# One of four weight sums of a quad made by two transfers instead of by VectorE

## The chip, the cores and the metric

The kernel runs on one core of a Trainium2 chip. The metric is the device time of one execution in microseconds (us). Before the change it is 1186.18 us, the median of two executions (1186.14 and 1186.23).

## What is computed

The reference is one layer of an encoder over 512 tokens of width 1024: a first feed-forward block, a mixer (attention beside an mLSTM), a second feed-forward block and a gated embedding. The change touches only the two feed-forward blocks:

```python
def swiglu(x, w_gate, w_up, w_down):
    return (jax.nn.silu(x @ w_gate) * (x @ w_up)) @ w_down

u = rmsnorm(h, ffn1_pre_norm[i])
h = h + 0.5 * rmsnorm(swiglu(u, ffn1_w_gate[i], ffn1_w_up[i], ffn1_w_down[i]), ffn1_post_norm[i])
# ... mixer ..., then the same with the ffn2 weights
```

w_gate and w_up are 1024 x 2816 and w_down is 2816 x 1024, all float32.

## The kernel before

**Precision.** Each float32 factor is split in two parts for TensorE: a high part (`w_hi`, a copy rounded by ScalarE) and a low part (`w_lo`, the difference, made by VectorE). A product is three matmuls, high by high, high by low and low by high.

**A feed-forward block** is built by `ffn`, called once for each block. Its gate and up weights are worked off in 11 pairs of 256 columns. The first two pairs (`LEADS`) are multiplied plainly. The other nine give 18 "quads", one of gate columns and one of up columns for each pair: 36 quads in the kernel. `w_down` follows.

**A quad** is a product of 2 x 2 blocks in the manner of Strassen and Winograd, with seven block products instead of eight. The weights of a quad lie in two slots of `w_raw`, one transfer of 512 KB each: the first holds rows 0 to 511 of 256 columns, the second rows 512 to 1023. `raw_blocks` names A11 and A21, the two column halves of the first slot, and A12 and A22, those of the second. Each is 128 partitions by 512 elements, 256 KB. VectorE makes four sums of them in `wsum` (`sum_dve`, lines 971 to 977):

S1 = A21 + A22, S3 = A11 - A21, S2 = S1 - A11, S4 = A12 - S2.

The operands of the seven products come in four groups g. Group 0 is A11, group 1 the whole second slot (A12 and A22), group 2 is S1 and S2, group 3 is S3 and S4. For each group ScalarE makes the high part (`group_hi`, line 910) and VectorE the low part (`group_lo`, line 923), in the order 0, 2, 3, 1. TensorE multiplies in `block_pe` (lines 781 to 783), seven products of 12 matmuls of 256 columns, and waits before its products for `s_lo` (low parts done) and `rcopy` (copies by ScalarE between banks): products 2 and 3 need group 2, product 4 group 1, products 5 and 6 group 3, product 7 group 1 and the fourth copy of its quad.

**The order on each engine is written out by hand**, and each engine works its queue in order. While TensorE multiplies quad qd, the other engines prepare quad qd + 1:

- VectorE (`dve_prog`): `group_lo` 0, then the sums S1, S3, S2 and S4, `group_lo` 2, three results of quad qd (lines 990 to 1001), `group_lo` 3, one more result, `close_dve`, `group_lo` 1.
- ScalarE (`act_prog`): copy 1 of quad qd, `group_hi` 0, copies 2 and 3, `group_hi` 2, which waits for S2, copy 4, `group_hi` 3, `group_hi` 1.
- SP (`sp_prog`, line 742) issues the two raw loads of quad qd + 2 as soon as all sums (`s_dve`) and low parts (`s_lo`) of quad qd are made.
- GpSimd (`pool_prog`) adds squares and makes `vraw` before the first quad (lines 593 to 596 and 1123) and has nothing to do in the quads.

Of the kernel before, what the change touches and what calls it, by code (L numbers as in the profile page):

```python
# [22 lines left out]
ALU = mybir.AluOpType  # L23
# [6 lines left out]
P = 128  # L30
# [29 lines left out]
LEADS = 2  # L60
# [60 lines left out]
def program(nc, w, const, out):  # L121
    ctx = ExitStack()
    with ctx:
        block_build(nc, w, const, out, ctx)


def block_build(nc, w, const, out, ctx):
# [151 lines left out]
    class Boundary:  # L279

        signals = Signals("boundary")
        PER = {"y_ready": (8, 7, 1, 7, 0), "y_copied": (0, 8, 8, 8, 0), "ysq_act": (0, 8, 8, 8, 8),
               "y_acc": (0,) + tuple(ADDED.values()), "y_sum": (0, 1, 1, 1, 1), "r1_ready": (0, 2, 1, 1, 1), "r1_root": (0, 1, 0, 0, 1), "r1b_ready": (0, 1, 1, 1, 1),
               "h_ready": (8,) * 5, "vhi_ready": (8,) * 5, "v_ready": (8,) * 5, "hsq_ready": (8,) * 5,
               "h_acc": (8,) * 5, "h2_ready": (1,) * 5, "r2_ready": (1,) * 5, "r2b_ready": (1,) * 5,
               "rb_ready": (1,) * 5, "t_ready": (0, 8, 8, 8, 0), "h_kept": (0, 8, 8, 8, 0)}
# [7 lines left out]
        def wait(self, eng, name, value):  # L294
            eng.wait_ge(self.signals[name], sum(self.PER[name][:self.n]) + value)

# [68 lines left out]
    def hi_upto(act, n):  # L365
        while hi_next[0] <= min(n, CHUNKS - 1):
            split_hi(act, hi_next[0])
            hi_next[0] += 1
# [219 lines left out]
    def h_squares_pool(pool, n, beside=None):  # L588
        b = bs[n]
        for m in range(KD):  # L590
            b.wait(pool, "hsq_ready", m + 1)
            if m == 0:
                nc.gpsimd.tensor_copy(sqacc[:], scratch[:, 0, :]).then_inc(b["h_acc"], 1)
            else:
                b.wait(pool, "h_acc", m)
                nc.gpsimd.tensor_tensor(sqacc[:], sqacc[:], scratch[:, m % 4, :], ALU.add).then_inc(b["h_acc"], 1)
            if beside is not None and m < 5:
                beside(m)
        if beside is not None:
            for m in range(5, KD):  # L600
                beside(m)
# [78 lines left out]
    class Block:  # L680

        signals = Signals("ffn")
        PAIRS = NI - LEADS
        PER = {"mm": 14 * PAIRS, "post": 8 * PAIRS, "rcopy": 8 * PAIRS, "s_dve": 8 * PAIRS, "s_hi": 8 * PAIRS,
               "s_lo": 8 * PAIRS, "lead_out": 4 * LEADS, "gate_scaled": NI, "silu_done": NI, "prod_ready": NI, "phi": KF,
               "plo": KF, "vraw_ready": KD, "t_raw": 4, "t_hi": 4, "t_lo": 4}

# [6 lines left out]
        def before(self, name):  # L694
            return self.n * self.PER[name]

# [3 lines left out]
    def ffn(n, N, DN, wg, wu, wd, pre):  # L700
        own = Block(n // 2)
        yb = bs[n + 1]
        QUADS = 2 * (NI - LEADS)
# [8 lines left out]
        def halves(ap):  # L712
            return ap.rearrange("p (k c) -> p k c", k=4)

        def raw_blocks(q):

            a, b = (halves(w_raw[:, (N + 2 * q + e) % RING, :]) for e in range(2))
            return a[:, :, 0:P], b[:, :, 0:P], a[:, :, P:2 * P], b[:, :, P:2 * P]

        def raw_loaded(qd, e):  # L720

            j = 2 * (qd % 2) + e
            return w_loaded[(N + j) % RING], LOADED[N + 4 * (LEADS - 1) + j] + 16 * (qd // 2 + 1)
# [13 lines left out]
        def sp_load(sp, i, j):  # L737

            m = N + j
            up, half = (j // 2, j % 2) if i > 0 else (j % 2, j // 2)  # L740
            src = (wu if up else wg)[0, half * 512:half * 512 + 512, i * 256:i * 256 + 256]
            sp.dma_start(w_raw[:, m % RING, :].rearrange("p (k c) -> p k c", k=4),
                         src.rearrange("(k p) c -> p k c", p=P)).then_inc(w_loaded[m % RING], 16)

        def sp_prog(sp, loaded=0, after_lead=None):
            for j in range(loaded, 4):
                if N + j >= RING:
                    sp.wait_ge(w_lo_done, N + j - RING + 1)
                sp_load(sp, 0, j)
            if after_lead is not None:  # L750
                after_lead(sp)
            for i in range(1, NI):
                for j in range(4):
                    if i <= LEADS:
                        sp.wait_ge(w_lo_done, N + 4 * (i - 1) + j + 1)
                    else:
                        qd = 2 * (i - LEADS - 1) + j // 2
                        own.wait(sp, "s_dve", 4 * qd + 4)
                        own.wait(sp, "s_lo", 4 * qd + 4)
                    sp_load(sp, i, j)  # L760
            for k in range(KF):
                m = DN + k
                if k < RING:
                    qd = QUADS - 2 + k // 2
                    own.wait(sp, "s_dve", 4 * qd + 4)
                    own.wait(sp, "s_lo", 4 * qd + 4)
                else:
                    sp.wait_ge(w_lo_done, m - RING + 1)
                sp.dma_start(w_raw[:, m % RING, :], wd[0, k * P:k * P + P, :]).then_inc(w_loaded[m % RING], 16)
# [114 lines left out]
        def group_ap(g, q):  # L884

            if g == 1:
                return w_raw[:, (N + 2 * q + 1) % RING, :], slice(0, CH)
            if g == 0:
                return raw_blocks(q)[0], slice(0, CH // 2)
            return wsum[:, 2 * g - 4:2 * g - 2, :, :].rearrange("p a k c -> p (a k c)"), slice(0, CH)  # L890

        S1, S2, S3, S4 = (wsum[:, a, :, :] for a in range(4))

        def group_hi(act, qd, g):

            if qd == QUADS:
                if g == 0:
                    hi_upto(act, DN)
                return
            if g < 2:  # L900
                act.wait_ge(*raw_loaded(qd, g))
            else:
                own.wait(act, "s_dve", 4 * qd + g + 1)
            if qd == 0:
                act.wait_ge(w_used, N + 4 * (LEADS - 1) + g + 1)
            else:
                own.wait(act, "mm", 7 * (qd - 1) + FREED[g])
            src, c = group_ap(g, qd % 2)
            o = w_hi[:, (N + g) % RING, c]
            nc.scalar.activation(halves(o) if g == 0 else o, src, ACT.Copy).then_inc(own["s_hi"], 1)  # L910
# [50 lines left out]
        def sum_dve(dve, qd, e):  # L961

            if qd == QUADS:
                return
            A11, A12, A21, A22 = raw_blocks(qd % 2)
            if e == 0:
                for r in range(2):
                    dve.wait_ge(*raw_loaded(qd, r))
                if qd >= 1:
                    own.wait(dve, "s_lo", 4 * (qd - 1) + 3)  # L970
                nc.vector.tensor_tensor(S1, A21, A22, ALU.add).then_inc(own["s_dve"], 1)
                nc.vector.tensor_tensor(S3, A11, A21, ALU.subtract).then_inc(own["s_dve"], 1)
                own.wait(dve, "s_dve", 4 * qd + 1)
                nc.vector.tensor_tensor(S2, S1, A11, ALU.subtract).then_inc(own["s_dve"], 1)
            else:
                own.wait(dve, "s_dve", 4 * qd + 3)
                nc.vector.tensor_tensor(S4, A12, S2, ALU.subtract).then_inc(own["s_dve"], 1)

        t0, t1 = slice(0, 256), slice(256, 512)
# [97 lines left out]
        def act_prog(act, late=None, arena_free=None):  # L1077
# [9 lines left out]
            if arena_free is not None:  # L1087
                arena_free(act)
            bs[n].wait(act, "h_acc", KD)
            group_hi(act, 0, 0)  # L1090
            lead_out_act(act, 1, 0)
            group_hi(act, 0, 2)
            silu_act(act, 1)
            group_hi(act, 0, 3)
            group_hi(act, 0, 1)
            lead_out_act(act, 1, 1)
# [23 lines left out]
        def pool_prog(pool):  # L1120

            def keep_raw(m):
                nc.gpsimd.tensor_tensor(vraw[:, m, :], h[:, m, :], pre(m).broadcast_to([P, S]), ALU.mult).then_inc(own["vraw_ready"], 1)

            h_squares_pool(pool, n, keep_raw)

        def y_wait(eng, p):
            if p < KD - 1:
                yb.wait(eng, "y_ready", p + 1)
            else:  # L1130
                eng.wait_ge(w_used, DN + KF)

        return sp_prog, pe_prog, dve_prog, act_prog, y_wait, sp_load, pool_prog

    f1 = ffn(0, UP1, DN1, w["ffn1_w_gate"], w["ffn1_w_up"], w["ffn1_w_down"], lambda m: col("ffn1_pre_norm", m))
    f2 = ffn(2, UP2, DN2, w["ffn2_w_gate"], w["ffn2_w_up"], w["ffn2_w_down"], lambda m: col("ffn2_pre_norm", m))

    def half_post(a):
# [1082 lines left out]
    block = ctx.enter_context(nc.Block())  # L2221
# [277 lines left out]
```

## Time and profile before

| | |
|---|---|
| median of the runs | 1186.18 us |
| the profiled execution | 1183.95 us |
| its span, first to last instruction | 1182.2 us |
| TensorE busy | 1170.5 us, 99% of the span |
| VectorE busy | 817.8 us, 69% |
| ScalarE busy | 582.5 us, 49% |
| GpSimd busy | 131.0 us, 11% |
| moved by transfers | 111.99 MB, mean 95 GB/s |
| mean granted TensorE clock | 0.996 of full speed |

The profile names an instruction by its line in the kernel, its engine, its operation and its tiles. Matmuls overlap, so their busy times add up to more than the time in which they follow each other. What an engine waited for stands behind its idle time. For transfers the profile gives the time from the issue on the queue to the landing of the last byte.

### The profile page before, as it was taken

To read this page: it belongs to the slowest core of one execution; us is meant where nothing else is said; L and a number is where in the kernel's file an instruction comes from. 1 tells how busy PE (TensorE), PEld (TensorE's weight loads), DVE (VectorE), ACT (ScalarE), POOL (GpSimd) and SP (SyncE) were. 2 spreads that over 40 slices of the span, in tenths; PEclk is the share of its full clock that TensorE was granted. 3 is DMA by queue.
4 is the path that set the end of the run, shared out by engine and by line. 5 is a ranking of instruction groups with operands and counts; after the bars stand their busy time and mean duration, and the time that the engine had idled before them with its cause. 6 is when DMAs were issued, how large, how long until landed. Compare 5 with 4: busy or idle time off the path is not lost.

```text
span 1182.2 us, 17769 instructions
## 1 busy us (share of the span) xinstructions
PE 1170.5 (99%) x6860; PEld 1009.6 (85%) x6860; DVE 817.8 (69%) x1309; ACT 582.5 (49%) x921; POOL 131.0 (11%) x111
## 2 busy tenths in 40 slices
PE   9999999999999999999999999999999999999998
PEld 8899999988888886667887888789999998888887
DVE  6888888773337787665466874688888886333574
ACT  6555555533236437666333623565555554323473
POOL 6000000000014000001022201430000000000344
PEclk9999999999999999999999999999999999999998
DMA  6233333342231331111532233322333334232211
GB/s 210 86 107 106 107 107 106 112 138 90 96 93 36 90 107 53 37 38 49 146 89 72 86 111 107 98 81 72 107 106 107 107 106 143 89 106 90 89 37 72
DMA packets 101854, 111.99 MB, mean 95 GB/s; under 512 B 15294, under 2 KB 91678, under 8 KB 101542
## 3 DMA queue, kind: packets, MB, share of 16 engines
q1 hardware_dynamic: 97542, 109.18, 29.8%
q10 hardware_dynamic: 4256, 2.12, 0.6%
q8 instruction: 29, 0.48, 0.2%
q14 instruction: 27, 0.22, 0.1%
HBM read 108.12 MB, written 3.16 MB: 94 GB/s over the span
## 4 chain that ended last, share of the span: by engine, by line
PE 91%; DVE 4%; ACT 3%; issue 2%; DMA 1%; SPq 0%; POOL 0%; ACTq 0%; DVEq 0%
PE bank L303 14%; PE bank L305 14%; PE bank L304 14%; PE bank L781 10%; PE bank L782 10%; PE bank L783 10%; PE bank L626 2%; PE bank L620 2%; PE bank L621 2%; PE bank L310 1%; PE bank L312 1%; PE bank L311 1%; PE bank L1366 1%; PE bank L455 1%; PE bank L1345 1%
## 5 line engine op out<-in xcount | busy, mean ns | idle before, releaser
L337 DVE TENSOR_TENSOR w_lo<-w_raw,w_hi 128x1024 fp32r<-128x1024 f32 x121 | 155.9, 1298 | 173.6 <-ACT w_hi L330 173.3
L330 ACT ACTIVATE w_hi<-w_raw 128x1024 fp32r<-128x1024 f32 x121 | 125.9, 1054 | 191.9 <-PE bank L305 183.1
L781 PE MATMUL bank<-T_hi,w_hi 128*128 128x256 f32 x576 | 163.1, 283 | 1.2 <-ACT bank L1075 1.2
L782 PE MATMUL bank<-T_lo,w_hi 128*128 128x256 f32 x576 | 163.0, 283 | 0.0
L783 PE MATMUL bank<-T_hi,w_lo 128*128 128x256 f32 x576 | 163.0, 283 | 0.0
L303 PE MATMUL bank<-T_hi,w_hi 128*128 128x512 f32 x352 | 137.3, 390 | 0.0
L304 PE MATMUL bank<-T_lo,w_hi 128*128 128x512 f32 x352 | 137.0, 389 | 0.0
L305 PE MATMUL bank<-T_hi,w_lo 128*128 128x512 f32 x352 | 137.0, 389 | 0.0
L303 PE MATMUL bank<-v_hi,w_hi 128*128 128x512 f32 x328 | 132.7, 405 | 0.0
L305 PE MATMUL bank<-v_hi,w_lo 128*128 128x512 f32 x328 | 128.2, 391 | 0.0
L304 PE MATMUL bank<-v_lo,w_hi 128*128 128x512 f32 x328 | 127.8, 390 | 0.0
L783 PE MATMUL bank<-v_hi,w_lo 128*128 128x256 f32 x432 | 122.3, 283 | 0.0
L782 PE MATMUL bank<-v_lo,w_hi 128*128 128x256 f32 x432 | 122.3, 283 | 0.0
L781 PE MATMUL bank<-v_hi,w_hi 128*128 128x256 f32 x432 | 122.2, 283 | 0.0
L923 DVE TENSOR_TENSOR w_lo<-wsum,w_hi 128x1024 fp32r<-128x1024 f32 x72 | 88.3, 1226 | 43.8 <-ACT w_hi L910 43.8
L910 ACT ACTIVATE w_hi<-wsum 128x1024 fp32r<-128x1024 f32 x72 | 76.4, 1061 | 83.2 <-PE bank L783 38.4
L781 PEld LDWEIGHTS bank<-T_hi,w_hi 128*128 128x128 f32 x576 | 110.6, 192 | 1.6 <-issue 1.6
L782 PEld LDWEIGHTS bank<-T_lo,w_hi 128*128 128x128 f32 x576 | 110.6, 192 | 0.0
L783 PEld LDWEIGHTS bank<-T_hi,w_lo 128*128 128x128 f32 x576 | 110.6, 192 | 0.0
L782 PEld LDWEIGHTS bank<-v_lo,w_hi 128*128 128x128 f32 x432 | 82.9, 192 | 0.1
L781 PEld LDWEIGHTS bank<-v_hi,w_hi 128*128 128x128 f32 x432 | 82.9, 192 | 0.1
L783 PEld LDWEIGHTS bank<-v_hi,w_lo 128*128 128x128 f32 x432 | 82.9, 192 | 0.0
(311 smaller groups left out, 2333.5 us busy)
## 6 DMA issues: line engine op xcount, KB each, us to landing
w_raw<-in_ffn_w_up SPq DMA_DIRECT2D x44, 512.0 KB, 4.0
w_raw<-in_ffn_w_down SPq DMA_DIRECT2D x44, 512.0 KB, 3.5
w_raw<-in_ffn_w_gate SPq DMA_DIRECT2D x43, 512.0 KB, 4.0
w_raw<-in_w_in SPq DMA_DIRECT2D x32, 512.0 KB, 3.7
w_raw<-in_w_out SPq DMA_DIRECT2D x8, 512.0 KB, 3.4
w_raw<-in_ple_w_gate SPq DMA_DIRECT2D x8, 512.0 KB, 3.4
x_tm<-in_x SPq DMA_DIRECT2D x4, 512.0 KB, 7.6
Mb<-m_rows ACTq DMA_DIRECT2D x8, 256.0 KB, 4.9
```

The costliest lines, as they stand in the source:

```text
L303: nc.tensor.matmul(o, whi, a_hi, start=start, stop=False)
L304: nc.tensor.matmul(o, whi, a_lo, start=False, stop=False)
L305: return nc.tensor.matmul(o, wlo, a_hi, start=False, stop=stop)
L330: nc.scalar.activation(w_hi[:, s, :], w_raw[:, s, :], ACT.Copy).then_inc(w_hi_done, 1)
L337: nc.vector.tensor_tensor(w_lo[:, s, :], w_raw[:, s, :], w_hi[:, s, :].bitcast(F32), ALU.subtract).then_inc(w_lo_done, 1)
L620: nc.tensor.matmul(o[:], whi, v_hi[:, k, :], start=(k == 0), stop=False)
L621: nc.tensor.matmul(o[:], wlo, v_hi[:, k, :], start=False, stop=False)
L781: nc.tensor.matmul(o, whi, a_hi(kk), start=(start and kk == 0), stop=False, skip_group_check=True)
L782: nc.tensor.matmul(o, whi, a_lo(kk), start=False, stop=False, skip_group_check=True)
L783: last = nc.tensor.matmul(o, wlo, a_hi(kk), start=False, stop=(kk == 3), skip_group_check=True)
L910: nc.scalar.activation(halves(o) if g == 0 else o, src, ACT.Copy).then_inc(own["s_hi"], 1)
L923: nc.vector.tensor_tensor(o, src, hh, ALU.subtract).then_inc(own["s_lo"], 1)
```

## The change

S1 is no longer made by VectorE. GpSimd issues two transfers for each quad. The first copies A21 from the weights in HBM to the place of S1 in `wsum`. GpSimd waits until it has landed and issues the second, which reads A22 from HBM and adds it to what lies in S1 (`accum_op=ALU.add`). Both move 256 KB in rows of 128 float32. Before the first one GpSimd waits until the low part of group 2 of the quad before is made (the last reader of the old S1 and S2) and until its S2 is made. VectorE now makes S3 first and then waits for the landing of the second transfer (`s_acc`) before S2. The count of `s_dve` for each quad falls from four to three, and the waits on it are renumbered.

```diff
-        PER = {"mm": 14 * PAIRS, "post": 8 * PAIRS, "rcopy": 8 * PAIRS, "s_dve": 8 * PAIRS, "s_hi": 8 * PAIRS,
+        PER = {"mm": 14 * PAIRS, "post": 8 * PAIRS, "rcopy": 8 * PAIRS, "s_dve": 6 * PAIRS, "s_acc": 32 * PAIRS, "s_in": 32 * PAIRS, "s_hi": 8 * PAIRS,
...
-                        own.wait(sp, "s_dve", 4 * qd + 4)
+                        own.wait(sp, "s_dve", 3 * qd + 3)
...
-                own.wait(act, "s_dve", 4 * qd + g + 1)
+                own.wait(act, "s_dve", 3 * qd + g)
...
                 if qd >= 1:
                     own.wait(dve, "s_lo", 4 * (qd - 1) + 3)
-                nc.vector.tensor_tensor(S1, A21, A22, ALU.add).then_inc(own["s_dve"], 1)
                 nc.vector.tensor_tensor(S3, A11, A21, ALU.subtract).then_inc(own["s_dve"], 1)
-                own.wait(dve, "s_dve", 4 * qd + 1)
+                own.wait(dve, "s_acc", 16 * qd + 16)
                 nc.vector.tensor_tensor(S2, S1, A11, ALU.subtract).then_inc(own["s_dve"], 1)
             else:
-                own.wait(dve, "s_dve", 4 * qd + 3)
+                own.wait(dve, "s_dve", 3 * qd + 2)
                 nc.vector.tensor_tensor(S4, A12, S2, ALU.subtract).then_inc(own["s_dve"], 1)
...
             h_squares_pool(pool, n, keep_raw)
+
+            def block(qd, half):
+                i = LEADS + qd // 2
+                src = (wu if qd % 2 else wg)[0, half * 512:half * 512 + 512, i * 256 + P:i * 256 + 2 * P]
+                return src.rearrange("(k p) c -> p k c", p=P)
+
+            for qd in range(QUADS):
+                if qd >= 1:
+                    own.wait(pool, "s_lo", 4 * (qd - 1) + 2)
+                    own.wait(pool, "s_dve", 3 * (qd - 1) + 2)
+                pool.dma_start(S1, block(qd, 0)).then_inc(own["s_in"], 16)
+                own.wait(pool, "s_in", 16 * qd + 16)
+                pool.dma_start(S1, block(qd, 1), accum_op=ALU.add).then_inc(own["s_acc"], 16)
```

## Rows read from the trace of the kernel before

**Rows 1.** The page: the span, and busy time by engine

```profile
span 1182.2 us, 17769 instructions
PE 1170.5 (99%) x6860; PEld 1009.6 (85%) x6860; DVE 817.8 (69%) x1309; ACT 582.5 (49%) x921; POOL 131.0 (11%) x111
```

**Rows 2.** The page: the chain that ended last, shares by engine

```profile
PE 91%; DVE 4%; ACT 3%; issue 2%; DMA 1%; SPq 0%; POOL 0%; ACTq 0%; DVEq 0%
```

**Rows 3.** Waits: who waited for whom, us in total, times, longest

```profile
PE bank L781 <- ACT bank L1075: 1.2, 2, 0.6
...
ACT w_hi L910 <- DVE wsum L974: 31.6, 34, 1.6
```

**Rows 4.** Windows: busy us of each engine in a stretch, PEclk, DMA share, GB/s

```profile
57.00:238.00 181.00, 180.38 (x1503) 180.20 (x1503) 155.84 (x229) 101.27 (x155) 0.00 (x0) 1.00 0.33 108
```

**Rows 5.** Groups of instructions: S1's line, count, busy us, mean ns

```profile
L971 DVE TENSOR_TENSOR wsum<-w_raw 128x512 f32<-128x512 f32 x36 | 24.6, 684 | 0.0
```

**Rows 6.** Timeline of VectorE in the first block: start us, us, line, [idle before]

```profile
124.40 1.23 DVE L923 TENSOR_TENSOR w_lo<-wsum,w_hi 128x1024 fp32r<-128x1024 f32 x1 [0.40 <-ACT w_hi L910]
...
129.73 1.82 DVE L923 TENSOR_TENSOR w_lo<-w_raw,w_hi 128x1024 fp32r<-128x1024 f32 x2
131.47 0.68 DVE L971 TENSOR_TENSOR wsum<-w_raw 128x512 f32<-128x512 f32 x1
132.07 0.69 DVE L972 TENSOR_TENSOR wsum<-w_raw 128x512 f32<-128x512 f32 x1
132.67 0.68 DVE L974 TENSOR_TENSOR wsum<-wsum,w_raw 128x512 f32<-128x512 f32 x1
133.39 0.69 DVE L977 TENSOR_TENSOR wsum<-w_raw,wsum 128x512 f32<-128x512 f32 x1
134.48 1.23 DVE L923 TENSOR_TENSOR w_lo<-wsum,w_hi 128x1024 fp32r<-128x1024 f32 x1 [0.40 <-ACT w_hi L910]
```

**Rows 7.** Timeline of ScalarE: group 2's high part, fourth copy, group 3's

```profile
123.31 1.06 ACT L910 ACTIVATE w_hi<-wsum 128x1024 fp32r<-128x1024 f32 x1 [0.89 <-DVE wsum L974]
124.93 0.37 ACT L1075 ACTIVATE bank<-bank 128x256 f32<-128x256 f32 x1 [0.56 <-PE bank L783]
126.43 1.06 ACT L910 ACTIVATE w_hi<-wsum 128x1024 fp32r<-128x1024 f32 x1 [1.13 <-PE bank L783]
```

**Rows 8.** Timelines of GpSimd and VectorE around the first quads of both blocks

```profile
26.44 5.01 POOL L1123 TENSOR_TENSOR vraw<-h,cols 128x512 f32<-128x512 f32 x3
50.20 0.69 DVE L974 TENSOR_TENSOR wsum<-wsum,w_raw 128x512 f32<-128x512 f32 x1
53.15 1.22 DVE L923 TENSOR_TENSOR w_lo<-wsum,w_hi 128x1024 fp32r<-128x1024 f32 x1
62.79 0.69 DVE L974 TENSOR_TENSOR wsum<-wsum,w_raw 128x512 f32<-128x512 f32 x1
...
776.62 4.02 POOL L1123 TENSOR_TENSOR vraw<-h,cols 128x512 f32<-128x512 f32 x3
799.25 0.68 DVE L974 TENSOR_TENSOR wsum<-wsum,w_raw 128x512 f32<-128x512 f32 x1
```

**Rows 9.** `Mb` (eight transfers issued by ScalarE, 256 KB each): time to landing

```profile
DMA to landing us min/median/max: 3.2/4.9/7.4
```

**Rows 10.** DMA queues, 569 to 582 us: packets, MB, share of 16 engines

```profile
q10 hardware_dynamic: 3618, 1.81, 49.1%
```

**Rows 11.** SP's issue of two raw loads, and their queue, 131 to 136 us

```profile
131.02 1.08 SPq L742 DMA_DIRECT2D w_raw<-in_ffn_w_up  x2
...
q1 hardware_dynamic: 1056, 1.05, 63.1%
```

**Rows 12.** Windows, columns as in Rows 4, around a fall of the clock

```profile
1106.00:1110.00 4.00, 3.99 (x28) 3.31 (x26) 1.48 (x3) 1.69 (x3) 1.25 (x1) 1.00 0.11 14
1110.00:1115.00 5.00, 5.00 (x20) 4.07 (x20) 3.41 (x14) 2.00 (x3) 0.00 (x0) 0.66 0.79 303
```

**Rows 13.** DMA issues: transfer, count, KB each, median us to landing

```profile
x_tm<-in_x SPq DMA_DIRECT2D x4, 512.0 KB, 7.6
```

More of the change, by code:

```diff
@@ L764, in sp_prog @@
                     qd = QUADS - 2 + k // 2
-                    own.wait(sp, "s_dve", 4 * qd + 4)
+                    own.wait(sp, "s_dve", 3 * qd + 3)
                     own.wait(sp, "s_lo", 4 * qd + 4)
```

## The prediction

> **What bounds the kernel now.** I read the busy times first. TensorE is busy for 1170.5 of 1182.2 us [rows 1], and the chain that ended last runs over it for 91% [rows 2]. The windows of the first block's quads say the same: 180.38 of 181.00 us, at full clock, while VectorE has 155.84, ScalarE 101.27 and GpSimd nothing [rows 4]. The waits say what is left to win: TensorE waited 1.2 us in two places for ScalarE's copies, in all 36 quads [rows 3]. One quad takes 10.08 us, from the low part of group 2 at 124.40 to the same at 134.48 [rows 6]. So VectorE is not the limit of the quads, and relief for it can only pay if it shortens something TensorE waits for.
>
> **What is removed.** 36 additions of 684 ns [rows 5]. They follow each other every 0.60 us [rows 6], so VectorE gets back 0.60 us for each quad, 21.6 us in all. ScalarE's high part of group 2 does wait for S2, 31.6 us in all [rows 3], and would start up to 0.6 us earlier. But its low part is finished at 125.63 (124.40 + 1.23). TensorE begins product 7 of the running quad when group 3's high part is let go, at about 126.4 [rows 7]; a product lasts 10.08 / 7 = 1.44 us, so product 2 of the next quad, the first that needs group 2, comes at 126.4 + 2.88 = 129.3, 3.6 us later. TensorE's own queue hides all of it. Worth: 0 us. Without that cover it would be at most those 21.6 us. The renumbered waits cost nothing, since the same instructions release them.
>
> **What is added, and what it lies beside.** GpSimd may issue the first transfer for the next quad when the low part of group 2 is made, at 125.63 us [rows 6]. The sum is wanted when S2 starts, at 132.67, or at 132.07 now that S1's slot on VectorE is gone. So there are 7.04 us in which the two transfers cost nothing; call what they take together, from the first issue to the second landing, L. They can't overlap, since the second waits for the first.
>
> If L is longer, a loop closes that has nothing of TensorE in it: low part of group 2, first transfer, second transfer, S2, high part of group 2, low part of group 2. Outside the transfers it takes 3.04 us (132.67 to 134.48 + 1.23 = 135.71) [rows 6]. The quad then takes L + 3.04 us instead of 10.08, so each one is late by L - 7.04.
>
> The first quad of a block escapes: GpSimd ends its last piece at 31.45 and S2 follows at 50.20; in the second block it is 780.64 and 799.25, over 18.6 us each time [rows 8]. The second quad has 62.79 - 54.37 = 8.42 us [rows 8], 1.38 more than the others. 17 quads of each block pay.
>
> **What is queued behind the wait.** On VectorE, S2, S4, the low part of group 2 and the results of the running quad stand behind it. On ScalarE, the high part of group 2 waits for S2, and behind that is the fourth copy, which TensorE needs for product 7 of the *running* quad. That is the first thing to be late. The copy starts at 124.93 and takes 0.37; product 7 starts about when group 3's high part is let go, 126.43; the high part of group 2 ends 0.56 us before the copy [rows 7]. So it may come 0.56 + 1.13, some 1.7 us later, once for each block, before TensorE stands. The raw loads on SP's queue go out when the quad before is finished, two quads ahead, and get later with it; they are not in the loop. GpSimd's queue holds nothing else until the quads are over.
>
> **The price of the transfers.** The trace shows no transfer issued by GpSimd and none that adds. Nearest in size, in rows of 512 bytes and in source are the eight that fill `Mb`: 3.2 us at the shortest, 4.9 in the median, 7.4 at the longest [rows 9]. For the first transfer I take the median, since preparing 512 pieces by GpSimd should cost more than the shortest case. The second must also read what it adds to. `Mb`'s queue had the 16 engines busy for 49.1% of 13 us with 3618 packets, 28.2 ns of one engine for a packet, so 512 packets take 0.9 us [rows 10]; I add that once. It also meets the raw loads. They are issued at 131.02, 5.4 us after the first transfer, and keep the engines busy for 63.1% of 5 us, 3.15 us [rows 11]. The second transfer starts at about 4.9 and shares the engines with them; I take half, 1.6 us. So the second takes 4.9 + 0.9 + 1.6 = 7.4 and L = 12.3 us. Below it is bounded by 3.2 + 3.2 + 0.9 = 7.3 us, above by the four slowest large loads, 7.6 each [rows 13], with both additions 7.6 + 7.6 + 0.9 + 3.15 = 19.3 us.
>
> The Trainium skill, in "DMA: Bandwidth & Descriptors", section "Anatomy of one DMA — SWDGE (gpsimd) path", prices a transfer issued by GpSimd at about 2.0 us and its bytes at 436 GB/s. For 256 KB that makes an estimate of 2.6 us each and 5.2 us for both, and the sum would be no change. No row here shows it, and 2.6 is under the 3.2 of [rows 9].
>
> **The sum.** L - 7.04 = 5.26 us for each late quad. For a block 17 x 5.26 = 89.4 us, less 1.38 (second quad) and 1.7 (the copy's slack), 86.3 us; for both, 172.7 us. The profiled execution would go from 1183.95 us (its span of 1182.2 and 1.75 around it) to 1356.6; the runs shown lie 2.2 us above it, so their median goes from 1186.2 to 1359 us.
>
> **Rivals.**
>
> *The transfers are hidden.* L stays under about 7.9 us: then 17 x 0.86 - 3.1 = 11.5 us for a block, 23 for both, is the most, within 2%. Its own time is 1186 us. For it: at their shortest the rows give 7.3 us, where only 2.7 us would be lost. Against it: both would have to be at the shortest of eight, without meeting the raw loads. This is the one that ends as not slower; the limit is L = 7.04. The skill's estimate above is this case.
>
> *They are slower than the rows allow for*, L above 16.5 us, by the work of preparing or by adding piece by piece. At the upper bound of 19.3 it would be 2 x (17 x 12.26 - 3.1) = 411 us, 1597 us. For it: nothing in the trace has this form. Against: it takes three times the median of [rows 9] and more.
>
> *The clock falls and TensorE becomes the limit.* The new idle time lies in one piece of 5.3 us ahead of product 7. The trace shows one fall with its cause near: one-column matmuls just before, then 0.66 over 5 us [rows 12], at most 3.4 us at 1.2 GHz. Such a stretch costs TensorE 1.7 us a quad, 11.8 in all, still under 15.3, so it is hidden. Only if the clock stayed at 1.2 GHz for over 10.5 us of each quad would it decide; at that clock throughout, a quad takes 20.2 us, and the sum is 2 x 17 x 10.08 = 343 us, 1529 us. But then TensorE has no idle time left, which speaks against it.
>
> *VectorE's relief shows as a gain.* It has at most TensorE's waits in the quads, 1.2 us [rows 3]: never 2%.
>
> **How the numbers follow.** The late loop with L from 8 to 16.5 us gets 0.73, hidden transfers 0.14, transfers above that 0.09, the clock 0.03, a gain over 2% 0.01. A difference of about 2% is what a measurement of this kernel can tell from no change, so: faster 0.01, same 0.14, slower 0.85. The likeliest case gives 1359 us. L = 8 gives 2 x (17 x 0.96 - 3.1) = 26 us, 1212; L = 16.5 gives 2 x (17 x 9.46 - 3.1) = 315 us, 1502. I leave the 0.14 of no change outside and part of the slow tail: the range is 1210 to 1500 us.
>
> **What the profile after would show.** Right, if in the quads VectorE waits ahead of S2 for a transfer into `wsum`, about 5.9 us each time, if TensorE is idle for some 5 us before product 7 with ScalarE's copy as the releaser, and if the low parts of group 2 follow each other every 15.3 us. The additions of line 971 are gone, GpSimd's queue shows 72 issues, and the bytes moved rise by 72 x 256 KB, 18.9 MB, to 131 MB. The step on the price is right if the first transfer lands in about 4.9 us and the second in about 7.4. The step on the loop is wrong if the period is anything but those two and 3 us. If the wait ahead of S2 is missing and the quad stays at 10.08 us, the transfers were hidden, and the forecast was wrong at their price. If the granted clock is low across the quads and TensorE is busy all through, the clock was the cause.

## The result and the profile after

The changed kernel takes 1305.59 us (median of two, 1304.41 and 1306.77) against 1186.18: 1.101 times the time before, 95% interval 1.096 to 1.105. It is 119 us slower.

The page of the changed kernel (span, busy time, and the chain that ended last), to be read against [rows 1] and [rows 2]:

```profile
span 1302.4 us, 17839 instructions
PE 1219.6 (94%) x6860; PEld 1053.3 (81%) x6860; DVE 796.5 (61%) x1273; ACT 576.4 (44%) x921; POOL 205.1 (16%) x183
...
q0 software_dynamic: 21888, 18.88, 8.4%
...
PE 53%; DMA 27%; DVE 11%; ACT 5%; issue 4%; SPq 0%; POOL 0%; ACTq 0%; DVEq 0%
DMA wsum<-in_ffn_w_up 14%; DMA wsum<-in_ffn_w_gate 12%; PE bank L303 12%; PE bank L305 12%; PE bank L304 12%; DVE w_lo L923 3%; ACT w_hi L910 3%; DVE wsum L973 2%; PE bank L626 2%; PE bank L620 2%; PE bank L621 2%; PE bank L310 1%; PE bank L312 1%; PE bank L311 1%; PE bank L1378 1%
```

TensorE's share of the chain fell from 91% to 53%. The lines of the quads' matmuls (781 to 783) are no longer among the costliest of it; the two transfers into `wsum` are, with 27%, and with them line 973 (S2), line 910 and line 923: the loop of the prediction. The new queue moved 18.88 MB.

The waits of the changed kernel (us in total, times, longest), against [rows 3]:

```profile
ACT w_hi L910 <- DVE wsum L973: 149.7, 34, 6.0
DVE wsum L973 <- DMA wsum<-in_ffn_w_up: 81.5, 17, 5.3
...
DVE wsum L973 <- DMA wsum<-in_ffn_w_gate: 71.7, 16, 5.6
PE bank L781 <- ACT bank L1074: 70.3, 34, 3.6
```

S2 waited 153.2 us for the landing, 33 times. TensorE stood 34 times, once for each of the 17 late quads of both blocks, for ScalarE's copy, 70.3 us in all, where before it was 1.2 us.

One turn of the loop, in the timelines of VectorE and GpSimd (start us, us, engine, line), against [rows 6]:

```profile
119.50 1.23 DVE L923 TENSOR_TENSOR w_lo<-wsum,w_hi 128x1024 fp32r<-128x1024 f32 x1 [0.40 <-ACT w_hi L910]
...
126.08 0.69 DVE L971 TENSOR_TENSOR wsum<-w_raw 128x512 f32<-128x512 f32 x1
131.62 0.69 DVE L973 TENSOR_TENSOR wsum<-wsum,w_raw 128x512 f32<-128x512 f32 x1 [4.86 <-DMA wsum<-in_ffn_w_gate]
...
133.43 1.22 DVE L923 TENSOR_TENSOR w_lo<-wsum,w_hi 128x1024 fp32r<-128x1024 f32 x1 [0.40 <-ACT w_hi L910]
...
121.02 0.77 POOL L1135 DMA_DIRECT2D wsum<-in_ffn_w_gate  x1 [8.93 <-DVE w_lo L923]
124.52 1.28 POOL L1137 DMA_DIRECT2D wsum<-in_ffn_w_gate  x1 [2.73 <-DMA wsum<-in_ffn_w_gate]
```

The low part of group 2 ends at 120.73, the first transfer goes out at 121.02, the second at 124.52, and S2 starts at 131.62: L is 10.9 us. With the 3.04 us of the rest the turn should be 13.9, and it is (119.50 to 133.43).

SP's raw loads, in its own timeline, go out 0.6 us behind the adding transfer:

```profile
125.13 0.92 SPq L742 DMA_DIRECT2D w_raw<-in_ffn_w_up  x2
```

The times to landing of the first transfer, then of the second (both in the same view, by line, us):

```profile
DMA to landing us min/median/max: 3.1/3.2/3.7
...
DMA to landing us min/median/max: 4.7/6.9/7.9
```

The window of the first block's quads (columns as in [rows 4]):

```profile
60.00:249.00 189.00, 161.77 (x1158) 159.55 (x1159) 113.96 (x168) 75.59 (x118) 27.46 (x27) 0.88 0.50 116
```

The granted clock fell from 1.00 to 0.88; in the turn shown above it is 0.50, the lower level (1.2 GHz), from 121 to 124 us, after TensorE had stood 1.90 us up to 119.89. A quad of 13.9 us holds 2.1 us of waiting (70.3 / 34) and 10.08 us of work at full clock; the remaining 1.7 us are put down to the low clock.

### The profile page after: what moved, and what is told of

Read it like the earlier page. It is cut to its first block, busy times and chain, and to the rows that moved or that the text cites. A ratio compares the mean times of both kernels' runs of the same rounds, so it can differ in the third digit from the quotient of the medians.

```text
span 1302.4 us, 17839 instructions
## 1 busy us (share of the span) xinstructions
PE 1219.6 (94%) x6860; PEld 1053.3 (81%) x6860; DVE 796.5 (61%) x1273; ACT 576.4 (44%) x921; POOL 205.1 (16%) x183
## 2 busy tenths in 40 slices
DMA packets 123742, 130.87 MB, mean 100 GB/s; under 512 B 16446, under 2 KB 111262, under 8 KB 123430
## 3 DMA queue, kind: packets, MB, share of 16 engines
q0 software_dynamic: 21888, 18.88, 8.4%
## 4 chain that ended last, share of the span: by engine, by line
PE 53%; DMA 27%; DVE 11%; ACT 5%; issue 4%; SPq 0%; POOL 0%; ACTq 0%; DVEq 0%
DMA wsum<-in_ffn_w_up 14%; DMA wsum<-in_ffn_w_gate 12%; PE bank L303 12%; PE bank L305 12%; PE bank L304 12%; DVE w_lo L923 3%; ACT w_hi L910 3%; DVE wsum L973 2%; PE bank L626 2%; PE bank L620 2%; PE bank L621 2%; PE bank L310 1%; PE bank L312 1%; PE bank L311 1%; PE bank L1378 1%
## 5 line engine op out<-in xcount | busy, mean ns | idle before, releaser
L781 PE MATMUL bank<-T_hi,w_hi 128*128 128x256 f32 x576 | 175.1, 304 | 70.3 <-ACT bank L1074 70.3
L783 PE MATMUL bank<-T_hi,w_lo 128*128 128x256 f32 x576 | 172.5, 299 | 0.0
L781 PE MATMUL bank<-v_hi,w_hi 128*128 128x256 f32 x432 | 134.3, 311 | 0.0
L782 PE MATMUL bank<-v_lo,w_hi 128*128 128x256 f32 x432 | 134.0, 310 | 0.0
L783 PE MATMUL bank<-v_hi,w_lo 128*128 128x256 f32 x432 | 133.4, 309 | 0.0
L782 PEld LDWEIGHTS bank<-T_lo,w_hi 128*128 128x128 f32 x576 | 120.0, 208 | 0.0
L783 PEld LDWEIGHTS bank<-T_hi,w_lo 128*128 128x128 f32 x576 | 119.9, 208 | 0.0
L973 DVE TENSOR_TENSOR wsum<-wsum,w_raw 128x512 f32<-128x512 f32 x36 | 24.9, 692 | 153.2 <-DMA wsum<-in_ffn_w_up 81.5
L781 PEld LDWEIGHTS bank<-v_hi,w_hi 128*128 128x128 f32 x432 | 95.8, 222 | 0.1
L782 PEld LDWEIGHTS bank<-v_lo,w_hi 128*128 128x128 f32 x432 | 95.5, 221 | 0.1
```

The source lines that it names most:

```text
L781: nc.tensor.matmul(o, whi, a_hi(kk), start=(start and kk == 0), stop=False, skip_group_check=True)
L782: nc.tensor.matmul(o, whi, a_lo(kk), start=False, stop=False, skip_group_check=True)
L783: last = nc.tensor.matmul(o, wlo, a_hi(kk), start=False, stop=(kk == 3), skip_group_check=True)
```

## The experiments

Theory: a quad lasts as long as the two transfers and 3.04 us more. Still open were what makes the second transfer twice as long as the first, whether the fallen clock is part of the cost, and whether the removed addition was worth anything.

| kernel | first, second transfer, median us | time, us | ratio to before |
|---|---|---|---|
| changed | 3.2, 6.9 | 1305.6 | 1.101 |
| e1, second copies | 3.2, 3.3 | 1190.6 | 1.006 |
| e2, raw loads later | 3.2, 4.8 | 1242.3 | 1.049 |
| e3, 24 idle matmuls | 3.2, 4.7 | 1287.6 | 1.087 |
| e4, GpSimd adds | none | 1186.1 | 1.000 |
| e5, two buffers | 3.3, 4.8 | 1184.9 | 1.000 |
| e6, first only | 3.2, none | 1186.2 | 1.001 |
| e7, half added | 3.2, 5.3 | 1257.3 | 1.061 |
| e8, first by SP | 2.8, 5.2 | 1235.3 | 1.042 |
| e9, 12 idle matmuls | 3.2, 6.9 | 1300.5 | 1.097 |
| e10, e8 and e2 | 2.9, 4.9 | 1227.8 | 1.036 |

**e5: the loop broken, the transfers kept.** Odd quads get another buffer for S1, and for S2 as well. The readers of S1 and S2 are changed to match, and before the first quad GpSimd waits until the block's last squares are read from that buffer; these lines are left out here:

```diff
-                if qd >= 1:
-                    own.wait(pool, "s_lo", 4 * (qd - 1) + 2)
-                    own.wait(pool, "s_dve", 3 * (qd - 1) + 2)
-                pool.dma_start(S1, block(qd, 0)).then_inc(own["s_in"], 16)
+                if qd >= 2:
+                    own.wait(pool, "s_lo", 4 * (qd - 2) + 2)
+                    own.wait(pool, "s_dve", 3 * (qd - 2) + 2)
+                pool.dma_start(s1(qd), block(qd, 0)).then_inc(own["s_in"], 16)
                 own.wait(pool, "s_in", 16 * qd + 16)
+                if qd >= 1:
+                    own.wait(pool, "s_acc", 16 * qd)
+                pool.dma_start(s1(qd), block(qd, 1), accum_op=ALU.add).then_inc(own["s_acc"], 16)
```

> Odd quads have their S1 in another buffer (the one for sums of squares, idle in the quads), so the transfers for a quad may start one quad earlier; transfers, sizes, issuer and bytes stay the same. Loop theory: the room for the two transfers grows from 7.0 to 17.1 us, more than the 10.9 they take, TensorE is the limit again and the time goes back to 1184 to 1190 us. Rival, the transfers slow other work by themselves (raw loads late, shared memory, GpSimd): the time stays above 1200 us. If VectorE's 0.6 us for each quad were worth something after all, it would be under 1184 us.

Measured: 1184.86 us, ratio 1.0002 (0.9991 to 1.0014). The same 72 transfers are there, with the same issuer and the same bytes. The first lands in 3.3 us, the adding one in 4.8 instead of 6.9: here the raw loads go out about 2.2 us after it (118.52 and 120.72) and not 0.6. The window of e5, same stretch as [rows 4], and its waits of TensorE:

```profile
57.00:238.00 181.00, 180.38 (x1503) 180.20 (x1503) 147.40 (x212) 101.16 (x155) 32.12 (x31) 1.00 0.59 152
...
PE bank L782 <- ACT bank L1088: 1.2, 2, 0.6
```

TensorE is busy for 180.38 us at full clock, as before, with more traffic (152 GB/s against 108 in [rows 4]). The shorter landing alone would not do this: e2 below has the same 4.8 us with one buffer and takes 1242 us. So the whole loss comes by way of the loop that the single buffer closes; outside it neither the traffic nor GpSimd's issues cost anything that can be measured.

**e4: the removal alone.** GpSimd makes S1 by one addition. It must also wait until both raw loads of the quad have landed (not shown):

```diff
+                A11, A12, A21, A22 = raw_blocks(qd % 2)
+                nc.gpsimd.tensor_tensor(S1, A21, A22, ALU.add).then_inc(own["s_acc"], 1)
```

> No transfer at all: GpSimd makes S1 itself with one addition of A21 and A22 when the low part of group 2 is made; VectorE's addition stays removed. It prices the removal alone. Theory: VectorE's 0.6 us a quad is hidden behind TensorE, and GpSimd's addition (about 1.3 us, the mean of its other additions of 512 elements) fits in the 7.0 us, so 1184 to 1188 us. Rival, the removal is worth something on the path: up to 21.6 us less, 1165 us. Rival, the two engines disturb each other: over 1190 us with VectorE's instructions longer than before.

Measured: 1186.12 us, ratio 1.0002 (0.9993 to 1.0012). Windows of e4, same stretch as [rows 4]:

```profile
57.00:238.00 181.00, 180.38 (x1504) 180.20 (x1503) 146.71 (x211) 101.92 (x155) 20.79 (x16) 1.00 0.34 107
```

VectorE's busy time fell from 155.84 to 146.71 us and TensorE's stayed at 180.38. The removed addition is worth nothing, as forecast. The last rival holds in a small part: 11 of VectorE's 72 low parts of sums took 1.25 to 1.82 us, where before none took over 1.23, and TensorE hides that too.

**e6: the first transfer alone.**

```diff
-                own.wait(pool, "s_in", 16 * qd + 16)
-                pool.dma_start(S1, block(qd, 1), accum_op=ALU.add).then_inc(own["s_acc"], 16)
```

> Only the first transfer is left, so S1 is A21 and the adding of A22 is left out. Loop theory: 3.7 us from the low part of group 2 to the landing are under the 7.0 us of room, the quad is back at 10.08 us and the time at 1184 to 1188 us. Rival, any transfer by GpSimd into the quads costs something of its own: over 1190 us.

Measured: 1186.24 us, ratio 1.0005 (0.9995 to 1.0015). 3.7 us lie within the 7.04 us of room, and the quad is 10.08 us again.

**e1: the second transfer copies.**

```diff
-                pool.dma_start(S1, block(qd, 1), accum_op=ALU.add).then_inc(own["s_acc"], 16)
+                pool.dma_start(S1, block(qd, 1)).then_inc(own["s_acc"], 16)
```

> The second transfer overwrites S1 with A22 instead of adding to it (so the weights' sum is left out; nothing else changes). Loop theory: the quad takes the two transfers plus 3.0 us, so each us that the second loses takes 34 us off 1305.6 us. If adding costs only the extra read of 256 KB, 0.9 us, the second falls from 7.1 (124.5 to 131.6 us in the trace of the changed kernel) to 6.2 us, the quad from 13.9 to 13.0 and the time to about 1275 us. Rival, adding is slow by itself: the second falls to the first one's 3.8 us or near it and the time to 1200 to 1215 us. Rival, only the meeting with the raw loads counts: no change, 1300 to 1306 us.

Measured: 1190.59 us, ratio 1.0057 (1.0034 to 1.008), lower than in any of the three cases. The guess of 0.9 us for adding fell, by this run: the second transfer lands in 3.3 us (median), so adding, with what it brings along, costs 3.6 us. Two copies just fill the room. S2 waits in e1:

```profile
132.32 0.69 DVE L973 TENSOR_TENSOR wsum<-wsum,w_raw 128x512 f32<-128x512 f32 x1 [0.64 <-DMA wsum<-in_ffn_w_gate]
```

Here SP's loads go out 1.5 us after the second transfer (129.01 and 130.55), so e1 takes away the adding and part of the meeting at once. The next run parts them.

**e2: the raw loads wait until the adding transfer has landed.**

```diff
                         own.wait(sp, "s_lo", 4 * qd + 4)
+                        own.wait(sp, "s_acc", 16 * (qd + 1) + 16)
                     sp_load(sp, i, j)
```

> The adding transfer no longer meets the two raw loads: SP issues them only when it has landed, some 6 us later than now and still 7 us before their first use. If the meeting is what makes the second transfer 7.1 us long, it loses 1.6 us (half of the 3.15 us in which the loads filled the engines) to 3.15 us, and the time falls by 34 times that, from 1305.6 to 1250 at the one end and 1200 at the other. Rival, the second is long by itself (adding, or preparing by GpSimd): 1300 to 1306 us.

Measured: 1242.27 us, ratio 1.049 (1.0462 to 1.0518), 63 us less than the change. The adding transfer alone lands in 4.8 us:

```profile
DMA to landing us min/median/max: 4.5/4.8/7.3
```

Taken as differences of the three medians, its 6.9 us are 3.3 for a copy, 1.5 for adding and 2.1 for meeting the raw loads. The quad lasts 11.7 us (121.54 to 133.23). The edit does not hold back the loads of `w_down`: in the first block they go out 0.5 us after the last adding transfer (244.74 and 245.26), and the last turn of each block takes 14.0 and 14.1 us. The queues of e2, in the stretch of one first transfer (3.8 us, where raw loads still run) and of one adding transfer (4.9 us), show what adding is (packets, MB, share of the 16 engines):

```profile
q0 software_dynamic: 80, 0.26, 23.4%
...
q0 software_dynamic: 528, 0.26, 44.0%
```

The copy moves its 256 KB in 80 packets and keeps the engines busy for 0.89 us (23.4% of 3.8). The adding transfer moves the same bytes in 528 packets and takes 2.16 us (44.0% of 4.9). These 1.3 us more of the engines' time are near the 1.5 us that it lands later. The number of packets is not what makes it long, as e8 shows.

**e7: only half is added.**

```diff
+                pool.dma_start(S1[:, 0:2, :], block(qd, 1)[:, 0:2, :], accum_op=ALU.add).then_inc(own["s_acc"], 16)
```

> The second transfer adds only 128 KB, half of A22 (the other half of S1 stays A21, so half of the adding is left out). If what adding costs more than copying grows with the bytes, the second transfer falls from 6.9 us by half of its moving time (2.1 us of all engines) and by part of the meeting with the raw loads: 4.9 to 5.9 us, the quad 11.9 to 12.9 us, the time 1237 to 1271 us. Rival, the price is a fixed one for each adding transfer: it stays near 6.9 us and the time at 1295 to 1306 us.

Measured: 1257.33 us, ratio 1.0607 (1.0586 to 1.0629), with the second at 5.3 us and the quad at 12.2, inside the range of the theory. So a fixed price for each adding transfer is ruled out. The run halves the bytes that are moved together with those that are added, so it does not show how much of the 1.6 us belongs to the adding and how much to the moving and the meeting.

**e8: SP issues the first transfer.**

```diff
+            sp.dma_start(wsum[:, 0, :, :], block(qd, 0)).then_inc(own["s_in"], 16)
...
                         qd = 2 * (i - LEADS - 1) + j // 2
+                        if j % 2 == 0:
+                            first_sp(sp, qd + 1)
```

> The first transfer is issued by SP on the hardware queue, ahead of the raw loads, the second stays with GpSimd. It prices GpSimd as the issuer. If preparing 512 pieces by GpSimd is costly, the first one falls from 3.2 us by 0.5 us or more and the time by 17 us or more, to 1288 us or less. If the issuer doesn't matter, the first one stays at 2.9 to 3.3 us and the time within 1295 to 1310 us.

Measured: 1235.26 us, ratio 1.0421 (1.0384 to 1.0458). The transfer is 0.4 us shorter (2.8 against 3.2), near the limit that I had set, but the time fell by 70 us, where 34 x 0.4 would be 14. The timelines of e8 show why:

```profile
127.65 1.28 POOL L1147 DMA_DIRECT2D wsum<-in_ffn_w_up  x1 [10.20 <-DMA wsum<-in_ffn_w_up]
...
128.92 0.98 SPq L742 DMA_DIRECT2D w_raw<-in_ffn_w_gate  x2
```

The adding transfer now goes out 1.3 us ahead of the raw loads instead of 0.6 and lands in 5.2 us instead of 6.9. Of its 528 packets 305 are through by 131 us, before the first packet of the raw loads; in the changed kernel the raw loads have moved 189 packets (126 to 128 us) before its own first one. The two savings, 0.4 + 1.7 us, times 34 make 71 us, which is the 70 measured. The expectation took the second transfer as fixed; it isn't, and its place against the raw loads is worth more than the issuer.

e8 also shows what SP's copy of A21 is, in a stretch of 3.1 us that holds nothing else (124.5 to 127.6):

```profile
q1 hardware_dynamic: 528, 0.26, 29.0%
```

It has 528 packets, as many as the adding transfer, and keeps the engines busy for 0.90 us, as the copy in 80 packets does. So the 2.16 us come with the adding and not with the packets.

**e10: e8 and e2 together.**

> The first transfer by SP (2.8 us) and the raw loads held back until the adding transfer has landed (4.8 us), both together. The loop worked out from its parts: 2.8 + 4.8 + 3.04 us and 0.7 us of releases (13.86 of the changed kernel less 3.2, 6.9 and 3.04) make 11.3 us a quad, 1.3 us over TensorE's 10.08; 34 x 1.3 less the 6 us of slack is 37 us, 1223 us, within 8. Rival, the two remedies act on the same thing and the meeting was all: no better than 1235 us.

Measured: 1227.84 us, ratio 1.0358 (1.0293 to 1.0423). The quad is 11.26 us in the mean of 15 turns of the first block, where the sum gave 11.3. The block's last turn is left out of that mean: it takes 13.9 us, since the loads of `w_down` aren't held back here either. The loop can be added up from its parts.

**e3 and e9: idle matmuls ahead of product 7**, 24 in e3 and 12 in e9.

```diff
+            for _ in range(24):
+                nc.tensor.matmul(B[4 * q][:, 256:512], v_hi[:, 0, 0:P], v_hi[:, 0, 0:256], start=True, stop=True,
+                                 skip_group_check=True)
             copied(4)
```

> 24 matmuls of 256 columns on idle data stand before product 7 of every quad, 24 x 0.12 = 2.9 us of TensorE's time into a bank region that nobody reads. Loop theory: TensorE is not in the loop, so with 10.1 + 2.9 = 13.0 us a quad it still has room under 13.9, the clock stays high over the quads (mean from 0.956 to 0.99 or more) and the time stays at 1303 to 1308 us. Rival, the clock is part of the cost: its low stretch costs TensorE some 1.7 us a quad, and with it gone the time falls by up to 58 us to about 1248 us. Rival, TensorE's time counts: the time rises by up to 36 x 2.9 = 104 us.

Measured: 1287.61 us, ratio 1.0873 (1.0843 to 1.0902). Neither case as written: the clock came back (mean 0.996), the kernel got 18 us faster, and the quad was 12.96 us, which is just TensorE's 108 matmuls of 0.12 us. So the loop had become shorter than 12.96. Its adding transfer lands in 4.7 us:

```profile
DMA to landing us min/median/max: 4.4/4.7/5.3
```

In e3's timelines it goes out at 120.44 and 133.36, the raw loads at 125.10 and 138.06, 4.7 us later. There were two readings: the clock paid, or the idle work had pushed product 7, group 1's low part and the raw loads away from the adding transfer. Half of the idle work tells them apart.

> The idle-data matmuls ahead of product 7 again, but 12 instead of 24: 1.4 us, so TensorE's quad is 11.5 us at full clock and stays well under the loop's 13.9, and product 7 isn't pushed back. It tells why 24 of them made the kernel 18 us faster. Theory: they pushed product 7, the low part of group 1 and so SP's raw loads back, away from the adding transfer (which fell from 6.9 to 4.7 us); 12 don't, so the adding transfer stays at 6 to 7.5 us and the time at 1295 to 1310 us. Rival, the kept clock was what paid: with the clock up and even less work added, the time falls to 1287 us or below.

Measured: 1300.49 us, ratio 1.0971 (1.0935 to 1.1006). Windows of e9, and its adding transfer:

```profile
60.00:249.00 189.00, 170.03 (x1383) 168.03 (x1384) 117.27 (x172) 78.51 (x123) 28.77 (x28) 0.99 0.50 120
...
DMA to landing us min/median/max: 4.7/6.9/7.7
```

The clock is at 0.99, the adding transfer at 6.9 us as in the changed kernel, and the time only 5 us lower, with intervals that overlap. The last 12 turns of the first block take 14.0 us in the mean, against 14.1 in the changed kernel at the lower clock. So the fall of the clock cost next to nothing. What the 5 us fit is short turns at the start of each block, three of 11.9 to 12.2 us in the first and two of 12.0 and 12.1 in the second. There the raw loads went out 1.3 to 1.7 us after the adding transfer, which landed in 4.7, 4.9 and 5.3 us in the three of the first block; in the long turns it is about 0.6, and 6.9 us. The other reading of e3's gain stands: its raw loads were moved away from the adding transfer, and its 4.7 us are near the 4.8 of e2, where nothing but that was changed.

## Why the prediction was right, point by point

- **The bound before, the removal worth nothing.** Right: e4, 1.0002.
- **The room of 7.04 us and the loop.** Right. Both sides were seen: e6 (3.7 us) is free, e1 (two copies) is at the edge with 1.006, and e5, which gives more room, is back at 1.000. The turn is L + 3.04 us, 13.9 where 15.3 was forecast, and S2 waits 4.6 us (153.2 / 33) where 5.9 was forecast. The text names another sign, a period of the two landings and 3 us. By that sign 0.8 us are missing: 3.2 + 6.9 + 3.04 is 13.1.
- **What is late first.** Right: TensorE stands ahead of product 7 for the fourth copy, 34 times. It is idle for 2.1 us each time and not for the 5 I named: some 1.7 us of the surplus went into the low clock, which I had in the text as hidden but not taken off the idle time, and L was shorter.
- **The price.** The sum was right in its make and 1.4 us too large in L: 12.3 forecast, 10.9 measured. The step that was mis-sized is the first term, the landing of one such transfer, 4.9 us taken from the median in [rows 9]. It is 3.2 us, the shortest of those rows. The eight went out in two groups of four; the first of the second group took 3.2 us, and the last of the first group 7.4, so that others in flight made the long ones long is likely, but no run tests it. The reason given for the median, the work of preparing 512 pieces, is worth 0.4 us (e8). For the second transfer I had 4.9 + 0.9 + 1.6 = 7.4, and it is 3.3 + 1.5 + 2.1 = 6.9: the base too large by 1.6, adding and the meeting too small by 0.6 and 0.5. The releases between the steps, some 0.8 us a turn (10.9 less 3.2 and 6.9), had no term at all. So two bases were 1.7 and 1.6 us too large, and three smaller terms together 1.9 too small. That the time came out as near as it did owes something to this.
- **The sum.** With L = 10.9 us it gives 34 x 3.85 less 6.2, 125 us; the span grew by 120.2. The 1359 us of the forecast less 34 x 1.4 is 1311, and 1305.6 was measured: a loss of 119 us where 173 was forecast.
- **The rivals.** Hidden transfers would have needed L under 7.9 us. The estimate by the Trainium skill ("DMA: Bandwidth & Descriptors", "Anatomy of one DMA — SWDGE (gpsimd) path"), 2.6 us a transfer, is under the 3.2 us that the trace shows for the copy; the adding and the meeting, 3.6 us together, come on top of that. The clock fell, as that rival said, but did not decide (e9). VectorE's relief gave nothing (e4).
- **The bytes.** 130.87 MB against 131 forecast, 72 issues.

## What to carry to other kernels

Before an engine's work is turned into transfers, draw the loop that its buffer closes and compare its length with the period of the bounding engine; here 10.9 us of transfers stood against 7.0 us of room, and a second buffer made them free. Two transfers of which one must wait for the other pay the full latency twice (3.2 and 3.3 us for the two copies of e1), and one that runs beside bulk loads pays for them too: where it stands against them in time can be worth more than who issues it. And work taken off an engine that isn't the bound buys nothing, so there was nothing here to set against the risk.

## What was not expected of the hardware

- A copy of 512 rows of 512 bytes issued by GpSimd moved in 80 packets and took 0.89 us of all engines; the same copy issued by SP moved in 528 packets and took 0.90 us; the adding transfer of the same shape moved in 528 packets and took 2.16 us. The count of packets tells nothing of the price here.
- GpSimd as the issuer cost only 0.4 us more than SP (3.2 against 2.8 us for the same transfer).
- TensorE's clock fell to 1.2 GHz for part of each quad (mean 0.88 of full speed over the quads) though it stood for only 2.1 us of 13.9 in the mean. Over the whole kernel the mean was 0.956; with 46.1 us of waiting in 33 pieces (e2, 1.4 us each) it stayed at 0.992.
- Adding idle work to the former bottleneck made the kernel 18 us faster (e3), by moving other engines' loads out of the way.
